# Two orders on VectorE: lower quarters of one weight slab among the index scores, and one feed-forward drain, in a hybrid decoder block

## The reference

```
h = rmsnorm(x)
q_sb,k_sb,v_sb | q_sa,k_sa,v_sa | q_idx,k_idx,w_idx | g_sb,g_sa = split(h @ W_in)
o_sb = stick_breaking(rmsnorm(q_sb), rmsnorm(k_sb), v_sb)        # 8 heads of 64
score[t,s] = sum_h w_idx[t,h] * relu(q_idx[t,h] . k_idx[s]) / sqrt(32)   # 8 index heads of 32, s <= t
idx = top_k(score, 128)                                          # per query
o_sa = softmax attention of 8 query heads, 2 key heads, over idx, with ALiBi
x = x + (sigmoid(g_sb) * (o_sb @ W_sb) + sigmoid(g_sa) * (o_sa @ W_sa)) @ W_out
x = x + relu(rmsnorm(x) @ W1)^2 @ W2
```

## Time and profile before

| | |
|---|---|
| median of 3 runs | 714.76 us (714.24 to 714.97) |
| profiled execution | 714.67 us |
| its span, first to last instruction | 712.9 us |
| TensorE busy (matmuls) | 707.0 us, 99% |
| VectorE busy | 555.2 us, 78% |
| ScalarE busy | 349.8 us, 49% |
| GpSimd busy | 225.8 us, 32% |
| chain that ended last, share of TensorE | 98% |

### The profile page before, as it was taken

One profiled execution on the slowest core, in us unless ns is written; L12 is line 12 of the kernel. 1 busy time (PEld: TensorE's weight loads), 2 busy tenths in 40 slices (PEclk: granted clock), 3 DMA queues, 4 the chain that ended last, 5 costly groups with the idle time before them and its releaser, 6 DMA issues.

```text
span 712.9 us, 9720 instructions
## 1 busy us (share of the span) xinstructions
PE 707.0 (99%) x3430; PEld 570.1 (80%) x3430; DVE 555.2 (78%) x801; ACT 349.8 (49%) x498; POOL 225.8 (32%) x184
## 2 busy tenths in 40 slices
PE   8999999999999999999999999999999999999998
PEld 5878878787777777788889888888888888888886
DVE  7354888999885885569986678694959778695897
ACT  6244653365666877832644453536244351634341
POOL 2005324002230000010131280907245180815587
PEclk9999999999999999999999999999999999999999
DMA  9408332312110312289353215051422405131103
GB/s 315 166 16 253 102 103 75 119 55 65 60 60 1 63 56 60 79 229 234 138 177 120 92 52 177 36 177 59 148 88 81 155 0 185 50 118 60 60 0 119
DMA packets 46150, 74.84 MB, mean 105 GB/s; under 512 B 2721, under 2 KB 27553, under 8 KB 46114
## 3 DMA queue, kind: packets, MB, share of 16 engines
q1 hardware_dynamic: 44528, 71.21, 30.7%
q0 software_dynamic: 1584, 3.15, 2.5%
q10 hardware_dynamic: 2, 0.00, 0.0%
HBM read 69.90 MB, written 2.10 MB: 101 GB/s over the span
## 4 chain that ended last, share of the span: by engine, by line
PE 98%; DVE 1%; ACT 1%; issue 0%; DMA 0%; ACTq 0%; DVEq 0%
PE ps L2148 8%; PE ps L2150 8%; PE ps L2149 8%; PE ps L2177 7%; PE ps L2179 7%; PE ps L2178 7%; PE ps L488 6%; PE ps L490 6%; PE ps L489 6%; PE ps L495 5%; PE ps L497 5%; PE ps L496 4%; PE ps L2132 2%; PE ps L2131 2%; PE ps L2133 2%; PE ps L2061 2%
## 5 line engine op out<-in xcount | busy, mean ns | idle before, releaser
L735 POOL TENSOR_TENSOR a_lo<-qo_sb,a_hi 128x512 fp32r<-128x512 f32 x56 | 93.6, 1698 | 35.3 <-ACT a_hi L1094 35.3
L2148 PE MATMUL ps<-b_hi,cut_hi 128*128 128x512 f32 (+1 forms) x280 | 104.0, 372 | 0.0
L2149 PE MATMUL ps<-b_lo,cut_hi 128*128 128x512 f32 (+1 forms) x280 | 103.9, 371 | 0.0
L2150 PE MATMUL ps<-b_hi,cut_lo 128*128 128x512 f32 (+1 forms) x280 | 103.8, 371 | 0.0
L1083 ACT ACTIVATE qo_sb<-ps 128x512 f32<-128x512 f32 x32 | 19.1, 598 | 127.2 <-PE ps L2150 81.0
L495 PE MATMUL ps<-cut_hi,a_hi 128*128 128x512 f32 x152 | 61.3, 404 | 0.0
L2150 PEld LDWEIGHTS ps<-b_hi,cut_lo 128*128 128x128 f32 x280 | 52.7, 188 | 9.1
L2149 PEld LDWEIGHTS ps<-b_lo,cut_hi 128*128 128x128 f32 x280 | 52.8, 188 | 9.0
L2148 PEld LDWEIGHTS ps<-b_hi,cut_hi 128*128 128x128 f32 x280 | 52.7, 188 | 9.0
L497 PE MATMUL ps<-cut_hi,a_lo 128*128 128x512 f32 x152 | 59.5, 392 | 0.0
L496 PE MATMUL ps<-cut_lo,a_hi 128*128 128x512 f32 x152 | 59.4, 391 | 0.0
(11 more groups left out here) (263 smaller groups left out, 1721.9 us busy)
## 6 DMA issues: line engine op xcount, KB each, us to landing
raw<-in_w_ff_dram SPq DMA_DIRECT2D x32, 1024.0 KB, 5.5
raw<-in_w_in_dram SPq DMA_DIRECT2D x16, 1024.0 KB, 5.7
gates<-in_x_dram SPq DMA_DIRECT2D x8, 512.0 KB, 6.2
raw<-in_w_out_dram SPq DMA_DIRECT2D x4, 1024.0 KB, 6.4
raw<-in_w_in_dram SPq DMA_DIRECT2D x4, 512.0 KB, 7.7
raw<-in_w_branch_sb_dram SPq DMA_DIRECT2D x2, 1024.0 KB, 5.1
raw<-in_w_branch_sa_dram SPq DMA_DIRECT2D x4, 512.0 KB, 6.0
qT_sa<-in_w_out_dram POOLq DMA_DIRECT2D x2, 1024.0 KB, 9.9
```

Source lines behind the costliest of these rows:

```text
L735: return pool.tensor_tensor(left_lo[:, q], left[q], left_hi[:, q].bitcast(F32), ALU.subtract).then_inc(l_lo, 1)
L2148: T.matmul(dst, w_hi[:, w], b_hi[:, k, a:b], start=(k == 0), stop=False)
L2149: T.matmul(dst, w_hi[:, w], b_lo[:, k, a:b], start=False, stop=False)
L2150: mm = T.matmul(dst, w_lo[:, w], b_hi[:, k, a:b], start=False, stop=(k == KD - 1))
```

## The change

VectorE's order changes at two places; nothing is added or removed.

First, the four quarters of slab 6's lower part no longer stand behind the scores of heads 16, 17, 18 and 19 but behind those of heads 15, 17, 19 and 21. Heads 15 and 21 belong to other calls of `index_scores`: quarter 0 comes before head sums 9 and head scaling 8, quarter 3 comes after head sums 10, head scaling 9 and score 20.

Second, in `dve_late` the drain of A22 (group 6) goes ahead of the lower part of S3's weights (group 7).

```
+            QSA_LOW = {15: 0, 17: 1, 19: 2, 21: 3}
+
             def index_scores(part, cut=None):
 
                 for u in range(4 * part, 4 * part + 4):
...
                     if cut is not None:
                         dve_cut(cut, u % 4, 4)
+                    if u in QSA_LOW:
+                        dve_cut(2 * QSA, QSA_LOW[u], 4)
...
                         for m in range(TB):
-                            index_scores(2 + m, 2 * g + 2 if m == 2 else None)
+                            index_scores(2 + m)
                             if m < 3:
                                 head_sums(4 * g + m)
                             if m in (1, 2):
...
                 drain(g, S4)
+                drain(g, A22)
                 right_low(g + 1, S3)
-                drain(g, A22)
                 t4_made(g + 1)
```

## The result

The changed kernel takes **719.29 us** (median of 6 runs, 717.58 to 721.18) against 714.88 us (714.24 to 715.22) for the kernel before in the same comparison: ratio 1.0066, 95% interval 1.0054 to 1.0078. That is slower by 4.4 us, where +2.1 us and at most 717.4 us were forecast. The sign is right; the size is not.

A forecast was written before the change was run, and what follows sets the result against it. TensorE, busy 707.0 of 712.9 us, was taken as the bound, with time lost or won only where it stops. +2.4 for slab 6 and -0.3 at S2 gave +2.1 us, 716.8 us; range 715.9 to 717.4.

The forecast's parts named there:

- term of +2.4 us: First matmul of slab 6: starts at 94.33 instead of 92.03 us, +2.30, plus 0.08 for restart spacing.
- allowance for GpSimd: Quarter 0 beside GpSimd's causal select: stretched by 0.1 us, bounds 0 and 0.42, so quarter 3 is done at 94.28.
- Two scores in a row: VectorE's index scores: a score directly behind a score takes 0.85 us, against 0.66 from a score to a quarter.
- Rival (B): Slab 6: delay partly absorbed or quarter 3 sooner, +0.8 to +1.6 us, 715.5 to 716.4 us; chance 0.14.
- Stops at heads 20 to 23: TensorE's index work: stops shrink from 1.05 us to about 0.3, the gain swallowed by the wait for slab 6.
- Rival (C): TensorE's stop ahead of slab 6: clock falls to 1.2 GHz, +1.25 us on top, 718.0 us; chance 0.04.
- The next instruction, `t4_made`, starts when it did: VectorE in `dve_late`: after the drain of A22 and lower part of S3 swap, the instruction behind them keeps its start.
- −0.30 with a bound of 0: TensorE's stop at product S2 of group 7 goes: 0.30 us gained, bounds 0 to 0.30.
- At the end of the span VectorE's last drain was idle for TensorE, so the 0.30 us reach the end: End of the span: the 0.30 us saved at product S2 shortens the whole kernel.
- The last sign of being wrong: Last part of the span: the forecast is wrong if stops of before turn out to be gone there.

The follow-up runs named there:

- early edit: Only the quarters of slab 6 moved behind heads 15, 17, 19, 21, against the kernel before: 718.17 us, ratio 1.0052, 6 runs.
- the one stretch traced: Quarters of slab 6 behind heads 15, 17, 19 and 23, drain of A22 unmoved, against the kernel before: 719.91 us, ratio 1.0074.
- the late edit alone: Only the drain of A22 moved ahead of the lower part of S3, against the kernel before: 715.85 us, ratio 1.0014.
- the six kept busy: The whole change plus 11 TensorE matmuls of zeros ahead of slab 6, against the kernel before: 716.44 us, ratio 1.0032, 6 runs.

## Why the prediction was right in sign and short in size

- **The early edit's mechanism and its term of +2.4 us: right.** Quarter 3 ran from 93.48 to 94.16 (start shift taken off) where 93.49 to 94.18, or 94.28 with the allowance for GpSimd, was forecast. Slab 6 came +2.52 − 0.33 = +2.2 us later, the restart spacing was 0.33 where 0.31 was forecast, and the runs at clock 1.000 give +1.9 to +2.4.
- **Quarter 0 beside GpSimd's select: the allowance of 0.1 was not needed**; it took 0.69 us.
- **Two scores in a row: 0.85 us as read**, and not the shorter step that the Trainium skill, "VectorE: DVE Perf Modes", section "The DRAIN you can't avoid", would give. Two of them are drawn 1.60 us long, (1.60 − 0.75) = 0.85. Rival (B), which leaned on it, falls.
- **Stops at heads 20 to 23: 0.37 us** with their restarts (0.13 at head 20, 0.24 at head 22), forecast 0.3, and the stop for slab 6 swallowed it as said.
- **Rival (C), the clock: under-weighted.** This is the first step that failed. The argument was that TensorE "is granted 0.9 or more even in the first slice, in which it starts from rest", and 0.04 was given. That digit was misread. Ahead of the first change of the grant the trace has no record of it, and the view then says 1.00. The matmuls say otherwise. The kernel after, busy time by stretch with the grant behind the five engines, and TensorE's timeline:

```profile
9.70:11.40 1.70, 1.70 (x5) 0.99 (x3) 1.26 (x2) 1.70 (x3) 0.75 (x2) 1.00 1.05 416
```

```profile
9.72 1.05 PE L1823 MATMUL ps<-cut_lo,a_hi 128*128 128x512 f32 x2
10.57 1.05 PE L1823 MATMUL ps<-cut_hi,a_lo 128*128 128x512 f32 x2
11.43 0.48 PE L1807 MATMUL ps<-cold_b,const_b 128*128 128x512 bf16 x1
```

The grant is given as 1.00, but pairs of matmuls begin 0.85 us apart, 0.43 for each: the lower level. In the trace of before the pair at 8.82 us comes 0.99 us ahead of the next, as the same pair does here (8.73, 9.72). TensorE starting from rest was no evidence against (C). And a slice is 17.8 us wide: where the clock fell for 6.8 us, one digit of 40 is 8 instead of 9. Its price was set at 1.25 us, for a stretch of work "as short as half the stop"; the one stretch traced, behind a longer stop, held 5.7 us of work. The three runs of the early edit with a fallen clock lie 2.2 to 3.3 us above the others; the four of both edits lie 1.5 to 3.6 us above the one at 1.000. What the Trainium skill says in "TensorE: Matmul & The Clock Gate", section "HAM oscillation — how this bites in real kernels", that waits between bursts of matmuls put the clock back, fits what was measured; the waits of its example are longer than the 1.80 and 2.65 us after which the clock fell in some runs here.
- **"The next instruction, `t4_made`, starts when it did": true, and not enough.** This is the second. It starts when it did and ends 1.1 us later. The late edit was costed by start times alone, −0.30 with a bound of 0, although the trace of before had the price of the new order: `t4_made` directly behind a lower part took 2.30 or 2.31 us in seven of seven cases, and 1.21 in the one case behind a drain (L1647 above). Lower parts themselves took anything from 1.20 to 2.32 us there, the long ones beside GpSimd. The Trainium skill, "SBUF — State Buffer", section "Who interferes with whom", says that a VectorE instruction with two SBUF inputs contends with a GpSimd instruction that reads SBUF, and that the pair of ports they share is an exclusive lock; 1.21 us that become 2.31 beside an instruction of GpSimd that takes 1.29 alone agree with it. A bound on the loss side of 1.1 us was to be had.
- **"At the end of the span VectorE's last drain was idle for TensorE, so the 0.30 us reach the end": this fell too.** The last drain is idle, but what ends the span is the queue of output transfers behind the drains before it. The tail was 3.15 us and became 4.60 in the traced execution (3.94 in that of the late edit alone), and with that the saved 0.3 us was lost several times over.
- **The last sign of being wrong contradicted the forecast.** It named stops of before that are gone in the last part of the span, which is what the late edit was forecast to do at S2, and did. The 0.44 us of the earlier trace rows are gone, and that says nothing against the forecast.

The terms for the median, then: +2.3 from slab 6, −0.3 from S2 and +1.45 from the tail make +3.5, if all are paid in one execution as in the traced one. The fallen clock comes on top in 4 of 6. That the median is +4.4 and not above +5 would fit runs in which the tail costs little, as in four of the six kept busy; of the six runs of the kernel after only the traced one shows what it paid. Of the steps that failed the clock weighs most in the median: kept busy, it falls to +1.8.

## What to carry to other kernels

A stop of TensorE costs its length and, with the stops of 1.8 to 4.4 us here, a chance of a slower stretch behind it: price the forecast stop at both clocks, and time the kernel in several runs, for a single profile may show none of it. When two instructions of VectorE are swapped, look not only at their starts but at which now stand side by side: of two in a row with both inputs in SBUF, beside a busy GpSimd, the second took nearly twice its time here; one drain from PSUM between them (0.6 us) did not help, two (1.2 us, about as long as GpSimd's instruction) did. And look at every execution of the instruction in the trace, not only at the one that the edit moves. And an order that saves time ahead of the last matmul has to be followed through the output transfers, whose issues had been spread out.

## What the hardware showed unexpectedly

- The granted clock fell in part of the executions of one and the same kernel: after stops of 1.80, 2.65 and 4.38 us in 2 of 10, 3 of 6 and 5 of 5 runs. The one stretch traced lasted 6.8 us at 0.50, from 1.0 us before the stop's end on. Filled with matmuls of zeros, a stop of that kind cost no clock in 13 runs.
- The start of an execution varies: head 20 comes at 87.75 to 88.82 us in 14 traces, and the offset is there by the first 50 us. In before the higher clock is granted from 9.93 us, in after from 11.62 us, and until then matmuls follow each other 0.43 us apart. In the 12 traces that record it, head 20 comes within 0.3 us of 88 us where the grant comes at 11 us or sooner; where the grant comes later, head 20 comes later too, up to 88.82 us with a grant at 12.67 us. That may be some of the spread of 1 us between runs of the kernel before.
- One of the last output transfers' issues takes 1.0 to 1.9 us instead of 0.33 in 12 of 14 traces, and ends just behind a read of 16 KB of instructions.
